# A two-block layer on one core: where the depthwise taps, the last weight units and a PSUM bank pair stand in the state-space stage

## The reference

```python
proj = rms_norm(x) @ w_in                  # glu 2x1024, z 2048, xBC 4096, dt 32, gates 2x1024
conv = silu(layer_norm(depthwise31(glu(proj.glu)))) @ conv_pw_w + conv_pw_b
xBC  = silu(depthwise4(proj.xBC))          # 8 groups: x 256 wide (4 heads of 64), B 128, C 128
for each chunk c, group g, head r:         # a_cs = cumsum(-exp(a_log) * softplus(dt + bias))
    diag  = (C B^T * exp(a_cs[l] - a_cs[s]) for l >= s) @ (x * dt)
    state = exp(a_end) * state + B^T (x * dt * exp(a_end - a_cs))
    off   = exp(a_cs) * (C @ state_before)
y = rms_norm_per_group((diag + off + d_skip * x) * silu(z)) @ ssm_out_w
mixed = (sigmoid(gate_conv + b) * conv + sigmoid(gate_ssm + b) * y) @ w_out
```

## Time and profile before

| | |
|---|---|
| runs | 2225.71 us median (2220.44, 2225.71, 2226.56) |
| the profiled execution | 2222.63 us, span 2220.9 us, mean granted clock 0.955 |
| busy over the span | TensorE 2019.8 us (91%), VectorE 1354.4 us (61%), ScalarE 1072.6 us (48%) |
| `groups` | about 1012 us to 1576 us of the span |
| transfers | 1 MB of A rows lands 4.9 us after its issue (median of 8) |

### The profile page before, as it was taken

The page is one execution under the profiler, slowest core; times in us unless marked ns, Lnnn a source line. Parts: engine busy times, 40 slices in busy tenths (PEclk is TensorE's granted clock), DMA queues, the critical chain, the costliest instruction groups (busy, mean ns, idle before and its releaser), DMA issues. The chain is left out here.

```text
span 2220.9 us, 24859 instructions
## 1 busy us (share of the span) xinstructions
PE 2019.8 (91%) x10049; PEld 1600.1 (72%) x10049; DVE 1354.4 (61%) x1513; ACT 1072.6 (48%) x1250; POOL 181.7 (8%) x131
## 2 busy tenths in 40 slices
PE   7999988699999999948999999988699979999997
PEld 5776767566666666627888888877488867888786
DVE  4113784699988988862598888876534543333222
ACT  4234613398888888843444444434242333222212
POOL 1002000023223223100000000000000000000000
PEclk9999999799999999977999999999899989999998
DMA  5210005399999999851433333222223213333221
GB/s 185 77 57 1 1 1 183 109 391 404 406 404 403 400 400 401 345 199 42 115 95 95 96 95 95 76 77 56 76 81 102 83 57 105 98 101 104 77 95 57
DMA packets 201775, 346.83 MB, mean 156 GB/s; under 512 B 13587, under 2 KB 149259, under 8 KB 184251
## 3 DMA queue, kind: packets, MB, share of 16 engines
q1 hardware_dynamic: 194459, 334.47, 43.0%
q0 software_dynamic: 5120, 8.40, 1.2%
q10 hardware_dynamic: 2080, 2.34, 0.3%
HBM read 340.91 MB, written 12.65 MB: 159 GB/s over the span
## 5 line engine op out<-in xcount | busy, mean ns | idle before, releaser
L1882 DVE TENSOR_TENSOR w_lo<-w_raw,w_hi 128x2048 fp32r<-128x2048 f32 x89 | 203.8, 2290 | 292.9 <-ACT w_hi L1874 292.8
L48 PE MATMUL pall<-hT,w_lo 128*128 128x512 f32 x864 | 345.0, 399 | 13.8 <-PEq L2004 5.1
L1874 ACT CAST w_hi<-w_raw 128x2048 fp32r<-128x2048 f32 x89 | 169.4, 1904 | 389.1 <-PE pall L50 370.6
L49 PE MATMUL pall<-hT,w_hi 128*128 128x512 f32 x864 | 339.5, 393 | 0.0
L50 PE MATMUL pall<-hT,w_hi 128*128 128x512 f32 x864 | 339.3, 393 | 0.0
L1582 DVE TENSOR_TENSOR wlo_e<-raw_e,hT 128x2048 fp32r<-128x2048 f32 x129 | 294.9, 2288 | 22.0 <-ACT hT L1504 21.9
L1504 ACT CAST hT<-raw_e 128x2048 fp32r<-128x2048 f32 x127 | 242.9, 1913 | 44.8 <-PE pall L1661 22.7
L1660 PE MATMUL pall<-hT,xs 128*128 128x512 f32 x512 | 205.8, 402 | 3.0 <-DVE xs L1587 3.0
L1661 PE MATMUL pall<-wlo_e,xs 128*64 128x512 f32 x512 | 202.2, 395 | 0.0
L48 PEld LDWEIGHTS pall<-hT,w_lo 128*128 128x128 f32 x864 | 164.5, 190 | 50.0 <-issue 8.2
L50 PEld LDWEIGHTS pall<-hT,w_hi 128*128 128x128 f32 x864 | 164.0, 190 | 34.9
(11 more groups left out here) (500 smaller groups left out, 3898.9 us busy)
## 6 DMA issues: line engine op xcount, KB each, us to landing
raw_e<-in_w_expert_up_dram SPq DMA_DIRECT2D x64, 1024.0 KB, 11.3
raw_e<-in_w_expert_gate_dram SPq DMA_DIRECT2D x64, 1024.0 KB, 11.9
w_raw<-in_w_expert_down_dram SPq DMA_DIRECT2D x61, 1024.0 KB, 11.8
w_raw<-in_w_in_dram SPq DMA_DIRECT2D x80, 512.0 KB, 6.0
w_raw<-in_w_gate_up_dram SPq DMA_DIRECT2D x44, 512.0 KB, 5.2
w_raw<-in_w_down_dram SPq DMA_DIRECT2D x22, 512.0 KB, 4.1
mixed<-in_w_in_dram SPq DMA_DIRECT2D x10, 1024.0 KB, 5.0
A<-acs_rows SPq DMA_DIRECT2D x8, 1024.0 KB, 4.9
```

The costliest lines, as they stand in the source:

```text
L48: nc.tensor.matmul(out, w_lo, m_hi, start=start, stop=False)
L49: nc.tensor.matmul(out, w_hi, m_lo, start=False, stop=False)
L1874: self.nc.scalar.copy(self.hi[i][:, :], self.raw[i][:, :]).then_inc(self.s_hi, 1)
L1882: (engine or self.nc.vector).tensor_tensor(self.lo[i][:, :], self.raw[i][:, :], self.hi[i][:, :].bitcast(F32), ALU.subtract).then_inc(self ...
```

## The change

What it does, in five parts:

1. **SP**: unit 32 (the first gate unit) is requested before the rows of A for group 7, not behind them.
2. **VectorE, groups 0 to 6**: there is a new place for taps, between `conv_taps` on x and the `make_lo` after it, and the table is new. Groups 0 to 6 now take 39, 28, 29, 35, 26, 33 and 26 taps (before 29, 22, 29, 25, 27, 27, 27).
3. **VectorE, group 7** is written out by itself: the decays come right behind `outputs(6)`, the `make_lo` of unit 33 moves behind `root(6)`, the `make_lo` of unit 34 behind the scores and four taps, that of unit 35 behind `outputs(7)`. Sixteen taps stand in it (before 22), and four are left after its root (before 28).
4. **TensorE**: the gate products alternate between banks 0, 1 and banks 2, 3. `ssm_gate(1)` waits for `outputs(6)` to have read banks 2 and 3, `ssm_gate(2)` for the read-out of `ssm_gate(0)`, `ssm_gate(3)` for `outputs(7)`; the off-diagonal part of group 7 waits for the read-out of `ssm_gate(1)`.
5. **The end**: ScalarE's `store(7)` comes before the read-out of `ssm_gate(3)`; `make_hi` and `make_lo` of unit 37 go to the start of `mix`.

```diff
-                until = unit_at["x", n + 1] + 1 if n + 1 < G else SG
+                until = unit_at["x", n + 1] + 1 if n + 1 < G else SG + 1
...
+        def gate_bank(u, j):
+            return banks[2 * (u % 2) + j]
...
-                    nc.scalar.activation(gs[2 * u + j], banks[j], ACT.Sigmoid, bias=col("gate_b", KD + 2 * u + j)).then_inc(s["gt"], 1)
+                    nc.scalar.activation(gs[2 * u + j], gate_bank(u, j), ACT.Sigmoid, bias=col("gate_b", KD + 2 * u + j)).then_inc(s["gt"], 1)
...
             ssm_gate(2)
             W.make_hi(act, SG + 4)
+            store(G - 1)
             ssm_gate(3)
-            W.make_hi(act, SG + 5)
-            store(G - 1)
...
-            SPREAD = [(4, 6, 5, 14), (0, 3, 3, 16), (5, 7, 5, 12), (4, 5, 4, 12)] + [(5, 7, 5, 10)] * 3 + [(8, 8, 6, 0)]
+            SPREAD = [(7, 4, 6, 5, 17), (0, 3, 3, 3, 19), (5, 4, 7, 5, 8), (4, 3, 5, 4, 19), (5, 3, 7, 5, 6), (5, 2, 6, 4, 16),
+                      (5, 3, 7, 5, 6)]
...
+            last = G - 1
+            outputs(last - 1)
+            decays(last)
+            root(last - 1)
+            W.make_lo(dve, ahead(last - 1, 3))
+            depthwise(6)
+            scores(last)
+            depthwise(4)
+            W.make_lo(dve, ahead(last, 0))
+            depthwise(4)
+            states(last)
+            depthwise(2)
+            outputs(last)
+            W.make_lo(dve, ahead(last, 1))
+            root(last)
+            depthwise(KD * CONV_K)
             W.make_lo(dve, SG + 4)
-            depthwise(8)
-            W.make_lo(dve, SG + 5)
-            depthwise(KD * CONV_K)
...
-                    pe.wait_ge(s["gt"], 2 * u)
+                    if u == 1:
+                        pe.wait_ge(s["yr"], G - 1)
+                    elif u == 2:
+                        pe.wait_ge(s["gt"], 2)
+                    else:
+                        pe.wait_ge(s["yr"], G)
...
+                else:
+                    pe.wait_ge(s["gt"], 4)
                 for c in range(1, C):
...
+            W.make_hi(act, CG + 1)
...
+            W.make_lo(dve, CG + 1)
```

More of the change, by code:

```diff
@@ L2473, in _, with decays @@
             depthwise(12)
-            SPREAD = [(4, 6, 5, 14), (0, 3, 3, 16), (5, 7, 5, 12), (4, 5, 4, 12)] + [(5, 7, 5, 10)] * 3 + [(8, 8, 6, 0)]
[L2475 to L2480, removed]
+            SPREAD = [(7, 4, 6, 5, 17), (0, 3, 3, 3, 19), (5, 4, 7, 5, 8), (4, 3, 5, 4, 19), (5, 3, 7, 5, 6), (5, 2, 6, 4, 16),
+                      (5, 3, 7, 5, 6)]
+            def decays(n):
                 dve.wait_ge(s["ar"], 16 * n + 16)
@@ L2494, in _, with scores @@
                 V.tensor_scalar(A[:, :, :], A[:, :, :], 0.0, None, ALU.min).then_inc(s["seg"], 1)
[L2495 to L2500, removed]
+            def scores(n):
                 dve.wait_ge(s["tx"], 2 * n + 2)
@@ L2519, in _, with states @@
                                 .to_broadcast([P, R, T]), ALU.mult).then_inc(s["A"], 1)
-                depthwise(spread[1])
+            def states(n):
                 if n >= 1:
@@ L2534, in _ @@
                         last.then_inc(s["stc"], 1)
+            for n in range(G - 1):
+                spread = SPREAD[n]
+                if n >= 1:
+                    outputs(n - 1)
+                    W.make_lo(dve, ahead(n - 1, 3))
+                decays(n)
+                if n >= 1:
+                    root(n - 1)
+                depthwise(spread[0])
+                conv_taps(n + 1, 0)
+                depthwise(spread[1])
+                W.make_lo(dve, ahead(n, 0))
+                scores(n)
+                depthwise(spread[2])
+                states(n)
                 W.make_lo(dve, ahead(n, 1))
-                depthwise(spread[2])
-                if more:
-                    conv_taps(n + 1, 2)
+                depthwise(spread[3])
+                conv_taps(n + 1, 2)
                 if n + 2 < KD:
@@ L2541, in _ @@
                     W.make_lo(dve, ahead(n, 2))
-                depthwise(spread[3])
-            outputs(G - 1)
-            root(G - 1)
+                depthwise(spread[4])
+            last = G - 1
[14 more added lines that the diff above has]
+            depthwise(KD * CONV_K)
             W.make_lo(dve, SG + 4)
-            depthwise(8)
-            W.make_lo(dve, SG + 5)
-            depthwise(KD * CONV_K)
         @block.tensor
@@ L2574, in ssm_gate @@
                 else:
-                    pe.wait_ge(s["gt"], 2 * u)
+                    if u == 1:
[4 more added lines that the diff above has]
+                        pe.wait_ge(s["yr"], G)
                 pe.wait_ge(*W.made(SG + u))
                 for j in range(2):
-                    product(nc, pe, W, SG + u, j, banks[j], hT)
+                    product(nc, pe, W, SG + u, j, gate_bank(u, j), hT)
             def turn_out(n):
```

## The result

| | before | changed |
|---|---|---|
| median of four runs | 2226.14 us (2220.44 to 2232.14) | 2187.08 us (2183.53 to 2190.44) |
| profiled execution | 2222.63 us, span 2220.9 | 2188.27 us, span 2186.5 |
| mean granted clock | 0.955 | 0.962 |

The ratio is 0.9839, with a 95% interval of 0.9821 to 0.9858: 1.6% faster. The changed kernel was timed again later, beside another one: 2188.74 us, ratio 0.9835 (0.9817 to 0.9854).

What follows compares the result with a forecast made beforehand. TensorE, busy 91%, was taken as the bound, judged by its waits; 17.7 + 5.1 + 18.0 + 2.4 - 6.2 = 37.0 us off gave 2185.6 (profiled) or 2188.7 (median), middle 2187; range 2180 to 2198.

Steps and rivals of the forecast that it cites:

- waits in and around groups 6 and 7: TensorE's waits of 9.0, 3.4, 4.0 and 1.5 us go, less 0.2 for small ones left: 17.7 us.
- half clock behind them: Stretches at 1.2 GHz behind TensorE's waits of 9.0, 3.4 and 4.0 us go: 5.1 us.
- the end of the stage: TensorE's 19.0 us wait before `mix` shrinks to ScalarE's last sigmoid and the crossing: 18.0 us go.
- half clock on the mean: The mean's matmuls behind the 19.0 us wait no longer run at reduced clock: 2.4 us.
- group 0: Added taps find almost no VectorE idle time there; TensorE loses 4.6 us plus 1.6 us restart: 6.2 us debit.
- The smallest margins: In groups 1 to 6, added taps fit VectorE's idle time, with smallest margins of 0.0 and 0.4 us.
- group 0's restart: TensorE's slow-clock cost behind its 6.7 us wait for xde: 1.6 us taken, between nothing and 1.9.
- The first: Rival: margins in groups 1 to 6 are absent, VectorE paces them, 13.7 us more: 2201; chance 0.08.
- the fourth: Rival: VectorE's chain has no slack in any group, waits for xde bring half clock: 2231, slower; chance 0.03.
- The second: Rival: ScalarE becomes late in group 7, with a half-clock restart, costing up to 6 us: 2193; chance 0.07.
- The third: Rival: part 1 does nothing, unit 32's load still late in group 6; 9.0, 1.9, 3.4 us stay: 2201; chance 0.04.
- The table load: ScalarE's function-table load takes 1.28 us by the profile row, preferred over the skill's 2.7 us with drain.

Runs made afterwards that it cites:

- e4: The kernel before with part 1 alone, unit 32 requested ahead of the rows of A; 2214.28 us, ratio 0.9954.
- e5: The changed kernel with group 0's ten added taps all at its end, before outputs(0), none before xde; one run, 2185.84 us.
- e6: The changed kernel with six taps more at the end of group 5, taken from group 7; one run, 2194.19 us.
- e10: The changed kernel with the taps of groups 0 to 6 dealt as before, thirty more left for the end; 2196.13 us, ratio 0.9872.
- e2: The changed kernel with part 4 undone, all gate products in banks 0 and 1 with the old waits; 2199.22 us, ratio 0.9883.
- e1: The changed kernel with part 1 alone undone, unit 32 requested behind the rows of A; 2198.25 us, ratio 0.9895.
- e3: The changed kernel with group 0's ten added taps taken out of it and put into group 7; 2182.58 us, ratio 0.9819.
- e9: The changed kernel with group 0 spared its ten added taps and ScalarE's first taps of the next x moved behind gate and normed; 2178.3 us, ratio 0.9799.

## Why the prediction was right

The time was forecast as 2187 and measured as 2187.08. Term by term, in the profiled executions:

| term | forecast | measured |
|---|---|---|
| waits in and around groups 6 and 7 | 17.7 | 17.4 (9.0 + 3.1 + 4.0 + 1.5, less the new 0.2) |
| half clock behind them | 5.1 | 5.1 (clock 1.00 from 1484.21 on) |
| the end of the stage | 18.0 | 18.0 (19.04 to 1.03) |
| half clock on the mean | 2.4 | 2.4 (clock 1.00, 7.1 us) |
| group 0 | -6.2 | -6.8 (4.6 + 2.2) |
| sum | 37.0 | 36.1 |

From the same early matmul of the stage to the end of the mean the traces differ by 36.7 us; 0.6 of them are in no term. The profiled executions as a whole differ by 34.4 us. The other 2.3 us lie where both programs do the same: the changed one reached that early matmul 1.1 us later, and took 1.2 us longer behind the mean, with more time at half clock there. The exact hit of the median is luck within that.

- **Part 1** was right in its chain and in its size, and two experiments say so from both sides (12 us undone, 10 us alone). The reason the taps at the end did not swallow it is the one expected for `e4`: a wait in VectorE's own queue delays those taps too.
- **Part 2** was right in the rule: `e5` and `e6` gave the waits of 6.7 and 2.6 us expected from it (6.62 and 2.60). The smallest margins held. VectorE's idle time before `make_lo` was 0.4 us in group 4, where I had counted none left, and before `outputs(3)` 0.8 us, where I had counted 0.4. The term that was mis-sized is group 0's restart: I took 1.6 us with 1.9 as the upper bound, it was 2.2 us in the profiled execution, and 2.2 to 2.9 in the seven traces that have this wait. Its bounds came from three single executions of other waits, and such a cost varies by itself.
- **Part 3** was costed by its chain, and the forecast gave it no term of its own; the one move tested gives 0.1 us. The 3.1 us of `turn_out(6)` come above all from the four taps fewer behind `conv_taps` in group 6, which belong to part 2 (`e10`).
- **Part 4** had the right wait, 4.0 us here and 4.4 us in `e2` (4.6 expected). Its restart was 1.7 us in the kernel before and 2.9 us in `e2`.
- **Part 5** I had costed at nothing, with the work that hides it, and that was right; but I gave it no credit for the short end of the stage, which rests on it: undone it costs 6.4 us, and the 18.0 us of the end are partly its doing.
- **The rivals.** The first and the fourth (VectorE paces the groups) fell with the waits of 0.8 us in groups 1 to 5. The second (ScalarE late in group 7) fell: no wait there is over 0.4 us. The third fell with group 6's rows.
- **The table load** of ScalarE behaved as its row: each load takes 1.28 us, and the instruction behind it starts at once. The Trainium skill (ScalarE: Activation LUTs, "What ACT_TABLE_LOAD costs") has the same for the load alone, and adds a drain of about 1.4 us, which no trace here shows. By an estimate from its figure `turn_out(6)` would have waited some 3 us, and it waited 0.31.

What the parts are worth, undone one at a time, is load 12 us, dealing of the taps in groups 0 to 6 9, bank pairs 7, end 6.4. These need not add up to 39 us: the parts share waits (the 9 hold a loss of 6.8 in group 0), and most of group 7's new order was not undone.

## What to carry to other kernels

A strand of filler work (here the taps) was free up to the idle time of its engine at that place, and counted in full beyond it, at both places where this was tried; so read the idle time before each wait and deal it out by that. Filler put where its engine has no idle time cost its whole length, plus a restart of TensorE, and nothing later returned it while TensorE was the bound. Before the end of a stage, look at what stands on each engine between the last product and the point where all engines meet: work that the next stage can hide behind its first matmuls belongs there.

## What the runs showed of the hardware

The restart of TensorE behind a wait is not a fixed price. Behind the same wait of 6.7 us in group 0 the same work took 14.5 us (the changed kernel) and 15.2 us (`e1`), against 12.3 at full clock. And half clock came behind much shorter waits than I had expected, in some executions: group 0's wait of 2.06 us in `e4` was followed by it, the same wait of 2.08 us in `e3` and in the kernel before was not. `e4`, the same stretch as above:

```profile
1119.43:1133.41 13.98, 13.98 (x55) 11.43 (x55) 13.77 (x23) 1.82 (x2) 0.00 (x0) 0.88 0.18 48
```

That is 1.7 us in one execution and none in another, and no run shows what decides it. It happened in three of the seven traces with a wait of about 2 us there (`e4`, `e9`, `e10`), and behind the waits of 0.8 us before `turn_out` in none of the traces. Such stretches are part of why runs of one kernel differ by some 7 us. Of the changed kernel there are two profiled executions, with spans of 2186.5 and 2189.8 us; in the longer one TensorE's matmuls lost 2.4 us more to half clock, nearly all of it outside groups 0 to 7, and its waits were 1.5 us longer.
